# Gate values through a DRAM table instead of one-hot matmuls, and first products ahead of second ones

## What is computed

```python
def _peer(h, w_query, sub_keys, expert_u, expert_v):
    q = (h @ w_query).reshape(B, S, PEER_HEADS, 2, PEER_KEY_DIM)          # 8 heads
    sc = jnp.einsum('bshpk,hpnk->bshpn', q, sub_keys)                       # 128 keys each
    v1, i1 = lax.top_k(sc[..., 0, :], 16)
    v2, i2 = lax.top_k(sc[..., 1, :], 16)
    cand = v1[..., :, None] + v2[..., None, :]
    top_s, pos = lax.top_k(cand, 16)
    idx = take(i1 * 128 + i2, pos)                                          # of 16384 experts
    g = jax.nn.softmax(top_s, axis=-1)
    act = gelu(einsum('td,tkd->tk', x, expert_u[idx]))
    out = einsum('tk,tkd->td', g * act, expert_v[idx])
```

## Time and profile before

| | |
|---|---|
| time, median of 3 runs | 1511.17 us (1507.37 to 1514.4) |
| the profiled execution | 1509.89 us |
| its span, first to last instruction | 1508.1 us |
| busy share PE, PEld, DVE, ACT, POOL | 97%, 86%, 59%, 54%, 38% |
| read from and written to DRAM | 242.50 MB and 7.34 MB |
| mean granted clock of TensorE | 0.997 of full speed |

### The profile page before, as it was taken

The page is one execution under the profiler, slowest core; times in us unless marked ns, Lnnn a source line. Parts: engine busy times, 40 slices in busy tenths (PEclk is TensorE's granted clock), DMA queues, the critical chain, the costliest instruction groups (busy, mean ns, idle before and its releaser), DMA issues.

```text
span 1508.1 us, 24377 instructions
## 1 busy us (share of the span) xinstructions
PE 1470.0 (97%) x8923; PEld 1302.1 (86%) x8923; DVE 889.2 (59%) x2185; ACT 819.0 (54%) x1483; POOL 576.4 (38%) x200
## 2 busy tenths in 40 slices
PE   7999999999999999989999999999999999999998
PEld 6788888788889898889999998888888888887886
DVE  4935259388336431225996662666666666667776
ACT  5556454488456644443556664555555555555554
POOL 6881665700467477456888884000000000000000
PEclk9999999999999999999999999999999999999999
DMA  8740435600334335333665334555555555556774
GB/s 332 274 169 29 167 129 177 225 30 2 108 121 163 140 141 183 121 143 113 197 211 153 98 105 161 196 195 194 185 185 189 193 195 195 186 189 219 243 241 163
DMA packets 60125, 251.08 MB, mean 166 GB/s; under 512 B 6144, under 2 KB 18560, under 8 KB 44160
## 3 DMA queue, kind: packets, MB, share of 16 engines
q1 hardware_dynamic: 60032, 249.86, 47.9%
HBM read 242.50 MB, written 7.34 MB: 166 GB/s over the span
## 4 chain that ended last, share of the span: by engine, by line
PE 66%; POOL 2%; ACT 2%; DVE 1%; issue 1%; DMA 0%; DVEq 0%; ACTq 0%
PE bank L1297 23%; PE bank L1321 9%; PE bank L702 6%; PE bank L869 6%; PE bank L1324 5%; PE bank L1250 4%; PE bank L705 3%; POOL wlo L1364 2%; PE bank L822 2%; PE bank L764 1%; PE bank L805 1%; ACT whi L1421 1%; PE bank L724 1%; PE bank L998 1%; PE bank L1150 1%; PE bank L980 1%
## 5 line engine op out<-in xcount | busy, mean ns | idle before, releaser
L1364 POOL TENSOR_TENSOR wlo<-raw,whi 128x2048 fp32r<-128x2048 f32 (+1 forms) x51 | 195.3, 3840 | 159.0 <-ACT whi L1421 158.7
L1364 POOL TENSOR_TENSOR wlo<-arena,whi 128x2048 fp32r<-128x2048 f32 (+1 forms) x45 | 195.1, 4342 | 151.1 <-ACT whi L1421 150.9
L1297 PE MATMUL bank<-whi,ghi 128*128 128x512 f32 x512 | 201.4, 393 | 3.6 <-DVE glo L2559 1.7
L1297 PE MATMUL bank<-wlo,ghi 128*128 128x512 f32 x512 | 201.0, 393 | 0.0
L1297 PE MATMUL bank<-whi,glo 128*128 128x512 f32 x512 | 200.0, 391 | 0.0
L1321 PE MATMUL bank<-hT,whi 128*128 128x512 f32 x624 | 154.3, 390 | 1.6 <-ACT whi L1767 1.6
L1321 PEld LDWEIGHTS bank<-hT,whi 128*128 128x128 f32 x624 | 117.0, 188 | 26.0 <-ACT whi L1767 1.8
L2516 DVE TENSOR_TENSOR wlo<-raw,whi 128x1024 fp32r<-128x1024 f32 x84 | 102.8, 1225 | 56.6 <-ACT whi L1774 56.6
L1377 POOL TENSOR_TENSOR wlo<-raw,whi 128x1024 fp32r<-128x1024 f32 x52 | 123.8, 2391 | 28.2 <-ACT whi L1717 28.1
L1421 ACT ACTIVATE whi<-arena 128x2048 fp32r<-128x2048 f32 x41 | 78.4, 1915 | 94.4 <-PE bank L822 28.7
L822 PE MATMUL bank<-whi,hT 128*128 128x512 f32 x512 | 125.8, 393 | 0.0
(11 more groups left out here) (336 smaller groups left out, 3027.0 us busy)
## 6 DMA issues: line engine op xcount, KB each, us to landing
raw<-ex_in SPq DMA_DIRECT2D x52, 1024.0 KB, 4.8
raw<-w_in SPq DMA_DIRECT2D x44, 1024.0 KB, 5.2
arena<-w_in SPq DMA_DIRECT2D x44, 1024.0 KB, 5.1
raw<-ex_in SPq DMA_DIRECT2D x84, 512.0 KB, 3.9
xw<-ex_in SPq DMA_DIRECT2D x26, 1024.0 KB, 4.7
xw<-ex_in SPq DMA_DIRECT2D x16, 512.0 KB, 4.0
arena<-spill SPq DMA_DIRECT2D x48, 128.0 KB, 3.8
spill<-gact SPq DMA_DIRECT2D x32, 128.0 KB, 3.7
```

The source lines that it names most:

```text
L1297: last = mm(bank[2 * t + h][:, :], g[:, j % 2, tok], w[:, b, at], start=False, stop=(final and i == 2), skip_group_check=True)
L1364: last = G.tensor_tensor(wlo[:, u % 2, at], slots[u % RING][:, at], whi[:, u % 2, at], ALU.subtract)
```

## The change

One-hot blocks, gate multiplications, the matmuls on them, the transposes of the selection, the spill and the main loop go. In their place:

- A DRAM table of 128 x 128 x 256 words (16 MB), W[second key][first key][token], is zeroed by sixteen 1 MB transfers from a zero tile, four at a time, on SP's queue behind weight units 19, 45, 63 and 79.
- VectorE computes for each token the expert number of each of its 128 slots and the place expert x 256 + token. `join` then sums, for slot s, the gates of all slots up to the end of its block of 16 that name the same expert, one instruction for each slot, with tokens in the partitions: 128 instructions for each token half. GpSimd sends each slot with an indexed transfer of 128 words (one for each token): 256 of these, one waiting for the landing of the earlier ones at each sixteenth. The last one to an expert carries the full sum.
- SP reads a tile's gates back from the table, 128 KB for a tile, 64 KB for a half.
- All first products are units of one list, with second products behind; quarters of the buffers turn in fours for all. 88 first products are in the early form, the rest merged. From tile 89 on, four in five tiles are followed by a half second product (token half 0 of tiles 0 to 31). The activations stay in SBUF.
- The low parts of the first 16 units are GpSimd's, the rest VectorE's. During the selection VectorE counts up the estimated us of what it has done (`spend`) and makes a low part at each 1.65 us. Of the eight score groups, six come before the first token half's selection, two behind its joins.

The core of the diff:

```diff
+UNITS = []
+for tile in range(N_KEYS):
+    UNITS.append(("first", tile, ()))
+    if visits_after(tile):
+        UNITS.append(("second", visits_upto(tile) - 1, (0,)))
+EARLY = visits_upto(N_KEYS - 1)
+FIRSTS = len(UNITS)
+for tile in range(EARLY, N_KEYS):
+    UNITS.append(("second", tile, (0, 1)))
+    if (tile - EARLY) % 2 == 1 and (tile - EARLY) // 2 < EARLY:
+        UNITS.append(("second", (tile - EARLY) // 2, (1,)))
...
+            for n in range(NU):                                   # SP
+                if n < 4:
+                    sp_.wait_ge(lo_ready, len(SPLIT_UNITS) - 3 + n // 2)
+                elif n - 4 < POOL_LOWS:
+                    sp_.wait_ge(u_lo_pool, n - 3)
                 else:
+                    sp_.wait_ge(u_lo_dve, n - 3 - POOL_LOWS)
+                kind, tile, some = UNITS[n]
+                sp_.dma_start(quarters[n % 4], ex_d[tile][:, 0:D] if kind == "first" else ex_d[tile][:, D:2 * D])\
+                   .then_inc(u_loaded[n % 4], 16)
+                if n - 1 in PLACE:
+                    m = PLACE[n - 1]
+                    _, tile, some = UNITS[n - 1]
+                    for t in some:
+                        sp_.wait_ge(scattered[t], 16 * SLOTS)
+                    if m >= 4:
+                        sp_.wait_ge(g_ready, m - 3)
+                    sp_.dma_start(w_ring[m % 4][:, tokens_of(m)], tiles_w[tile][:, tokens_of(m)]).then_inc(w_in[m % 4], 16)
...
+            def second_ready(n):                                  # TensorE
+
+                pe.wait_ge(glo_ready, PLACE[n] + 1)
+                low_ready(n)
...
+            for t in range(TT):                                   # GpSimd
+                pool.wait_ge(places_ready, t + 1)
+                if t > 0:
+                    pool.wait_ge(scattered[0], 16 * SLOTS)
+                for s in range(SLOTS):
+                    if s > 0 and s % 16 == 0:
+                        pool.wait_ge(scattered[t], 16 * s)
+                    pool.wait_ge(value_ready, SLOTS * t + s + 1)
+                    G.indirect_dma_start(table, bass.IndirectOffsetOnAxis(ap=places[:, t, s:s + 1], axis=0),
+                                         values[:, t, s:s + 1], None).then_inc(scattered[t], 16)
...
+            def unit_hi(n):                                       # ScalarE
+                if n >= NU:
+                    return
+                act.wait_ge(u_loaded[n % 4], 16 * (n // 4 + 1))
+                if n < 4:
+                    act.wait_ge(proj_done, 2 * NCHUNK - 1 + n // 2)
                 else:
+                    act.wait_ge(u_done, n - 3)
+                A(hi4[n % 4], quarters[n % 4], ACT.Copy).then_inc(u_hi, 1)
...
+            for n in range(NU - 2):
+                kind, tile, some = UNITS[n]
+                act.wait_ge(u_done, n + 1)
+                if kind == "first":
+                    if tile < MERGED:
+                        gelu(tile, first_bank(tile)[:, 0:T])
+                    else:
+                        A(act_at(tile), first_bank(tile)[:, T:2 * T], ACT.Copy).then_inc(b_taken, 1)
+                unit_hi(n + 4)
+                if kind == "first" and tile >= MERGED:
+                    act.wait_ge(sum_ready, tile - MERGED + 1)
+                    gelu(tile, first_bank(tile)[:, 0:T])
+                if n + 2 in PLACE:
+                    act_hi(PLACE[n + 2])
...
+            def join(t, at):                                      # VectorE
+
+                for s in range(at.start, at.stop):
+                    if s >= 2:
+                        dve.wait_ge(value_ready, SLOTS * t + s - 1)
+                    some = slice(0, 16 * (s // 16 + 1))
+                    V.scalar_tensor_tensor(I16ps[:, SLOTS * (s % 2):SLOTS * (s % 2) + some.stop], expert[:, some],
+                                           expert[:, s:s + 1], KPS[:, some], ALU.is_equal, ALU.mult,
+                                           accum_out=values[:, t, s:s + 1]).then_inc(value_ready, 1)
+                    spend(0.3)
...
+            for n in range(lows[0] - 4, NU - 2):
+                kind, tile, _ = UNITS[n]
+                if kind == "first" and tile >= MERGED:
+                    dve.wait_ge(b_taken, tile - MERGED + 1)
+                    out = first_bank(tile)[:, 0:T]
+                    V.tensor_tensor(out, out, act_at(tile), ALU.add).then_inc(sum_ready, 1)
+                if n + 4 < NU:
+                    unit_lo()
+                if n + 2 in PLACE:
+                    act_lo(PLACE[n + 2])
+                if n + 3 in PLACE:
+                    weigh(PLACE[n + 3])
```

More of the change, by code:

```diff
@@ L29, with visits_after, visits_upto @@
 PH = 8
[L30 to L55, removed]
+SLOTS = PH * 16
+POOL_LOWS = 16
+MERGED = 88
+VISITS = 32
+EXP_AT = (7, 56)
+def visits_after(i):
+    return 1 if i >= MERGED and (i - MERGED) % 5 > 0 and visits_upto(i - 1) < VISITS else 0
+def visits_upto(i):
+    return min(VISITS, sum(1 for j in range(MERGED, i + 1) if (j - MERGED) % 5 > 0))
+UNITS = []
[9 more added lines that the diff above has]
+        UNITS.append(("second", (tile - EARLY) // 2, (1,)))
+NU = len(UNITS)
+SECONDS = [n for n, (kind, _, _) in enumerate(UNITS) if kind == "second"]
+PLACE = {n: m for m, n in enumerate(SECONDS)}
 SCALE = HD ** -0.5
@@ L1284, in act_tile @@
[L1284 to L1292 removed]
+                elif i > 2:
+                    pe.wait_ge(act_ready, i - 2)
@@ new lines, in first_product, with low_ready, out_part @@
+                low_ready(n)
+                for k in range(KT):
+                    last = mm(out[:, 0 if i < MERGED else 1], l[:, k, :], hThi[:, k, :], start=False, stop=(k == KT - 1))
+                last.then_inc(u_done, 1)
+            def low_ready(n):
+                by_pool, by_dve = lows_before(n + 1)
+                if by_dve:
+                    pe.wait_ge(u_lo_dve, by_dve)
+                else:
+                    pe.wait_ge(u_lo_pool, by_pool)
+            def out_part(n, t, final, columns=range(2)):
+                m = PLACE[n]
@@ L1293, in out_part @@
                 for h in columns:
-                    at = slice(half.start + CW * h, half.start + CW * h + CW)
+                    at = slice(CW * h, CW * h + CW)
                     tok = slice(P * t, P * t + P)
-                    for i, (g, w) in enumerate(((ghi, whi), (ghi, wlo), (glo, whi))):
-                        last = mm(bank[2 * t + h][:, :], g[:, j % 2, tok], w[:, b, at], start=False,
+                    for i, (g, w) in enumerate(((ghi, hi4), (ghi, lo4), (glo, hi4))):
+                        last = mm(bank[2 * t + h][:, :], g[:, m % 2, tok], w[n % 4][:, at], start=False,
@@ new lines, in _ @@
+            for n in range(NU - 2):
+                kind, tile, some = UNITS[n]
+                if kind == "first":
+                    first_product(n, tile)
+                else:
+                    second_ready(n)
+                    for t in some:
+                        last = out_part(n, t, False)
+                    last.then_inc(u_done, 1)
+            for n in (NU - 2, NU - 1):
+                second_ready(n)
+                if n < NU - 1:
+                    out_part(n, 0, False, (0,))
@@ new lines, in _ @@
+            for q, t in ((0, 0), (0, 1), (1, 0), (1, 1), (2, 0), (3, 0)):
+                scores_of(q, t)
+            dve.wait_ge(tokens_ready, 1)
+            step(V.tensor_copy(token_f, token_u))
+            V.tensor_copy(iota16ps, tb("iota16", KEEP, keep))
+            dve.wait_ge(x_kept, 1)
+            select(0)
+            spent[0] = 1.65
+            join(0, slice(0, SLOTS))
+            scores_of(2, 1)
+            scores_of(3, 1)
+            select(1)
+            dve.sem_inc(selected, 1)
```

516 lines of the change are left out of this document (134 added, 382 removed).

## The result

The changed kernel takes 1583.0 us (median of 4 runs, 1581.2 to 1588.1), the kernel before 1509.4 beside it: a ratio of 1.049, 95% interval 1.045 to 1.053. The forecast was 1505 with a range up to 1580, so it was wrong in its point and, by 3 us, in its range; the rival called late gates came true on top of the forecast's own case.

What follows compares the result with a forecast made beforehand. TensorE's own work bounds the kernel. Second products could start at 1131.5; plus 4 for merged firsts, 361.5 for second products with waits and 5.7 for the end gives 1502.7, execution 1504.5, rounded to 1505 us; 8 in 10: 1492 to 1580.

Steps and rivals of the forecast that it cites:

- late gates: Rival, chance 0.20: indexed transfers at 1.6 us all-in end 45 late, SP and all later loads wait: 1550; at 1.72, 1580.
- the forecast's own case: Whole kernel: waits at the halves give back 56 of 66 us, gates in time; 1505, by itself 1494 to 1515, chance 0.45.
- the bound of 1.43: Indexed transfers on GpSimd: all-in price in us up to which 256 of them, from 763, end by 1128.
- The wait at the halves: Second products: TensorE idles about 1.5 us for glo ahead of the whole tile behind each half, 32 times.
- The chain: Second products: from unit n's end through high part, low part and glo until TensorE can begin n+2, 2.98 us.
- the triple: Second products: a half unit and two whole ones take 8.44 us in place of 6.82, 32 times.
- the last tiles: Last 32 whole second products: 2.855 us each by pairs of 2.73 + 2.98, 91.4 in all.
- the merged firsts: Forty merged first products with 32 halves among them: chain 4.67 against 4.13, at most 9 us lost, 4 taken.
- TensorE's own work: Whole kernel if nobody is late: TensorE ends at 1437, the execution takes 1444, 66 below.
- No wait at the halves: Rival, chance 0.14: in the second products the lead is longer, TensorE sets the pace: 1444 and turns, 1450.
- Falling clock: Rival, chance 0.12: waits of 1.5 us at the halves lower TensorE's clock, every second one costing 1.6, 26 us: 1531.
- VectorE and GpSimd block each other: Rival, chance 0.09: beside transfers VectorE's low parts wait 0.6 each, turn 3.24, 0.37 too long 73 times, 27 us: 1532.

Runs made afterwards that it cites:

- the order's second form: Changed kernel with the activations' high part, glo and the gate multiplication moved ahead of the weights' next parts: 1514.2 us, 1.0024 of the kernel before.
- the first form of the edit: Changed kernel with only the activations' high part (ScalarE) and glo (VectorE) moved ahead of the weights' next parts: 1587.3 us.

## Why the prediction was wrong, by its steps

**The step that failed: the price of an indexed transfer.** The prediction took it as 1.2 us all-in, the middle between 0.43 and 2.0, and so late gates at no cost; it measured 1.67, and the late gates cost 62 us. The bounds held, the choice didn't; the argument was that fifteen in sixteen aren't awaited. In fact issuing alone takes 1.26, waited for or not, above the 1.2 by itself; VectorE's low parts add 0.19 and the landings 0.18. The 1.26 alone would have been in time (763 + 323 = 1086); with either addition it is 1.44 to 1.45, past the bound of 1.43. Over 256 transfers the miss is 119 us, and the slack had been 58 (1128 less 1070). The start was 7 us late as well, 770.1 in place of 763. During the first selection GpSimd's low parts held up four of VectorE's operations, which took 2.3 to 2.45 us each (0.22 to 0.40 in the second selection, when GpSimd subtracts nothing); one of them:

```profile
742.64 2.44 DVE L2329 TENSOR_SCALAR arena<-arena 128x128 uint32<-128x128 uint32 x1
```

The earlier trace rows had shown this for one operation, and I used it for the rival and not for the time at which the selection ends.

**The rival late gates, by its own formula:** 1505 + (1196.4 - 1128) = 1573. Its mechanism, its place and its rule (SP waits, and all loads behind it) were right; its price of 1.6 was near, its chance of 0.20 too low. TensorE waited 48 instead of 68, since it was itself 20 us later by then. What it missed was the first half, wanted at 972 and there at 988.6: 11.8 us.

**The wait at the halves was right to a tenth.** The chain was forecast as 2.98 us and measures 2.99 (the tile ahead of the half ends at 1245.14, 0.23 behind the start of its last matmul, and the tile behind the half begins at 1248.13); the triple as 8.44 and takes 8.57; the last tiles 2.855 and take 2.92. 56 us were forecast to be lost here, and 61 came back behind the long wait with the order's second form. Here the wording fell short: "glo behind the low part" is one of two orders that cost this; the first form of the edit undid that one only and gained nothing.

**The sum.** Forecast span 1502.7, measured 1579.4. The gates: 11.8 + 47.6, and 2.8 of low clock behind them (matmuls of 0.63 in place of 0.39, starts 0.43 apart in place of 0.23, for some six and eight of them). The start of the stage and the early firsts 1.6, the merged firsts 9 where I took 4 (my upper bound was 9), the triples 32 x 0.13 = 4, the last tiles 2. That is 75 of 77.

**Other steps.** TensorE's own work was forecast as 1444 and is 1449.7. *No wait at the halves* was refuted by the timeline. *Falling clock* too, for the changed kernel: behind the waits of 1.2 us the matmuls take 0.50 and 0.39, as at full clock; only behind the two long waits do they take 0.63, and the granted clock in the window of the second is 0.61 on average. *VectorE and GpSimd block each other* happened, but its victim was not the one I named: VectorE's low parts beside transfers take 1.23 us as ever, and GpSimd pays. The early firsts came each 2.88 us. Of the zeroing the windows before 724 show a DMA share of 0.48 in place of 0.40 and TensorE as busy as before (696.7 and 696.9 us); the stage begins 1.2 us later, and whether that is the zeroing wasn't tried. The Trainium skill, page "DMA: Bandwidth & Descriptors", section "Anatomy of one DMA — SWDGE (gpsimd) path", has about 2.0 us fixed for a transfer: as a price for GpSimd's time it would be too high (1.26 here), and what GpSimd awaited behind each sixteenth was 3.3 on average (49.6 for fifteen).

## What to carry to other kernels

A series of small indexed transfers is a queue with a rate: multiply the issue price by the count and lay the end against the date on which the first reader wants it, before asking what else it replaces. For each product ask which of its inputs is made last and what stands ahead of that on its engine, and follow the chain past the first engine; an order that is mended at one link can close a ring at the next. A long wait that can't be removed can be filled; count what the filling work does to the chain that is awaited, here 13 us, and what it asks of the loads.

## What the runs showed that I had not expected

- An indexed transfer of 128 words occupies GpSimd for 0.96 us and the next one begins 0.30 later, whatever the waits. With an operation of VectorE on two inputs in SBUF beside it, it ends about 0.83 after that operation, so that it takes up to 2.0; beside copies out of PSUM it stays at 0.96.
- Instructions that should have been back to back came late on TensorE, in four kernels at one time, while indexed transfers were in flight; the loss was 94 to 218 us.
- At 296 to 304 GB/s (a share of 0.89 to 0.92) ScalarE began to wait for 512 KB loads, 7 to 8 us in sum; at 280 GB/s and 0.87 it didn't.
